# One GpSimd instruction instead of eight for the low part of a weight slot, in a two-block network on one Trainium2 core

## What is computed

```python
def rwkv7_time_mix(h, ...):
    hh = h_prev - h
    r = (h + hh * mu[0]) @ w_r
    k = (h + hh * mu[2]) @ w_k
    v = (h + hh * mu[3]) @ w_v
    g = sigmoid((h + hh * mu[5]) @ g1) @ g2
    ...

def swiglu_ffn(h, w_gu, w_down):
    gate, up = jnp.split(h @ w_gu, 2, axis=-1)
    return (jax.nn.silu(gate) * up) @ w_down

def reference(x, ...):
    x = first_block(x, ...)   # layer 0: rwkv7 + ffn; layer 1: differential attention + ffn
    return second_block(x, ...)  # layer 0: gla + spatial gating; layer 1: retention + pooling
```

## Time and profile before

| | |
|---|---|
| median of 3 runs | 2076.11 us (2075.34 to 2078.84) |
| the profiled execution | 2074.83 us, of which its span is 2072.8 us |
| TensorE (PE) busy | 1907.4 us, 92% |
| VectorE (DVE) busy | 811.7 us, 39% |
| ScalarE (ACT) busy | 764.0 us, 37% |
| GpSimd (POOL) busy | 776.3 us, 37% |
| mean granted TensorE clock | 0.972 of full speed |

### The profile page before, as it was taken

The page is one execution under the profiler, slowest core; times in us unless marked ns, Lnnn a source line. Parts: engine busy times, 40 slices in busy tenths (PEclk is TensorE's granted clock), DMA queues, the critical chain, the costliest instruction groups (busy, mean ns, idle before and its releaser), DMA issues.

```text
span 2072.8 us, 35505 instructions
## 1 busy us (share of the span) xinstructions
PE 1907.4 (92%) x14984; PEld 1563.6 (75%) x14984; DVE 811.7 (39%) x1297; ACT 764.0 (37%) x1046; POOL 776.3 (37%) x640
## 2 busy tenths in 40 slices
PE   5998988778999999999999799999999999989997
PEld 3666857667788888877677478888888877788876
DVE  5578433456332221017876532222102222423443
ACT  5776333433332222124256532222212323243232
POOL 3444400014434444435431144434445342334452
PEclk8999999998999999999999999999999999999998
DMA  5111100003233332322211023333223221132111
GB/s 173 62 34 61 40 3 4 3 24 103 62 102 101 90 93 97 112 76 92 71 52 42 13 80 91 101 101 96 96 97 97 82 82 41 41 107 82 62 61 62
DMA packets 192357, 149.58 MB, mean 72 GB/s; under 512 B 6890, under 2 KB 190401, under 8 KB 192228
## 3 DMA queue, kind: packets, MB, share of 16 engines
q1 hardware_dynamic: 192228, 147.68, 23.2%
HBM read 145.57 MB, written 2.10 MB: 71 GB/s over the span
## 4 chain that ended last, share of the span: by engine, by line
PE 73%; DVE 11%; issue 7%; ACT 6%; POOL 4%; DMA 0%; DVEq 0%; SPq 0%; ACTq 0%; POOLq 0%
PE psum L2686 20%; PE psum L2688 19%; PE psum L2687 19%; PE psum L2865 4%; POOL w_lo L1213 4%; ACT w_hi L1347 2%; PE psum L3164 1%; PE psum L3177 1%; DVE X_lo L1919 1%; DVE xf L2379 1%; DVE col L2428 1%; DVE tq L2399 1%; PE psum L3274 0%; PE psum L3057 0%; PE psum L3287 0%
## 5 line engine op out<-in xcount | busy, mean ns | idle before, releaser
L1213 POOL TENSOR_TENSOR w_lo<-weight_raw,w_hi 128x256 fp32r<-128x256 f32 (+5 forms) x597 | 731.0, 1257 | 1033.7 <-ACT w_hi L1347 1033.6
L2686 PE MATMUL psum<-X_hi,w_hi 128*128 128x512 f32 x1336 | 548.6, 411 | 33.0 <-DVE X_lo L1919 20.2
L2688 PE MATMUL psum<-X_hi,w_lo 128*128 128x512 f32 x1336 | 525.3, 393 | 0.0
L2687 PE MATMUL psum<-X_lo,w_hi 128*128 128x512 f32 x1336 | 524.8, 393 | 0.0
L1347 ACT ACTIVATE w_hi<-weight_raw 128x2048 fp32r<-128x2048 f32 (+1 forms) x136 | 252.9, 1860 | 294.5 <-PE psum L2688 294.4
L2686 PEld LDWEIGHTS psum<-X_hi,w_hi 128*128 128x128 f32 x1336 | 253.1, 189 | 112.5 <-issue 46.9
L2687 PEld LDWEIGHTS psum<-X_lo,w_hi 128*128 128x128 f32 x1336 | 253.5, 190 | 58.0 <-issue 8.9
L2688 PEld LDWEIGHTS psum<-X_hi,w_lo 128*128 128x128 f32 x1336 | 253.2, 190 | 55.0
L2686 PE MATMUL psum<-w_hi,X_hi 128*128 128x256 f32 x640 | 186.7, 292 | 10.3 <-POOL w_lo L1213 10.2
L2687 PE MATMUL psum<-w_lo,X_hi 128*128 128x256 f32 x640 | 182.3, 285 | 0.0
L2688 PE MATMUL psum<-w_hi,X_lo 128*128 128x256 f32 x640 | 182.1, 285 | 0.0
(11 more groups left out here) (473 smaller groups left out, 2593.1 us busy)
## 6 DMA issues: line engine op xcount, KB each, us to landing
weight_raw<-in_ffn_w_gu SPq DMA_DIRECT2D x88, 512.0 KB, 4.9
weight_raw<-in_l_w_in SPq DMA_DIRECT2D x45, 512.0 KB, 4.5
weight_raw<-in_ffn_w_down SPq DMA_DIRECT2D x40, 512.0 KB, 3.7
weight_raw<-in_kv_w SPq DMA_DIRECT2D x16, 512.0 KB, 4.4
weight_raw<-in_l_w_out SPq DMA_DIRECT2D x16, 512.0 KB, 4.4
weight_raw<-in_rw_w_o SPq DMA_DIRECT2D x12, 512.0 KB, 4.5
weight_raw<-in_rw_w_k SPq DMA_DIRECT2D x8, 512.0 KB, 6.7
weight_raw<-in_rw_w_r SPq DMA_DIRECT2D x8, 512.0 KB, 4.0
```

The costliest lines, as they stand in the source:

```text
L1213: ins = pool.tensor_tensor(l, r, h.bitcast(F32), ALU.subtract)
L2686: pe.matmul(ps, wh, xh, start=start, stop=False, skip_group_check=True)
L2687: pe.matmul(ps, wh, xl, start=False, stop=False, skip_group_check=True)
L2688: return pe.matmul(ps, wl, xh, start=False, stop=stop, skip_group_check=True)
```

## The change

`low_product`, slots 0 and 1, and slots 2 and 3 call `low` with `cut=False`:

```diff
             def low_product(name):
                 for i in range(sum(1 for q in PL.slots if q[0] == name)):
-                    low(PL.first_slot[name] + i)
+                    low(PL.first_slot[name] + i, cut=False)
...
-            low(0)
-            low(1)
+            low(0, cut=False)
+            low(1, cut=False)
...
             for n in range(2, 4):
-                low(n)
+                low(n, cut=False)
             for name in ("r", "g1", "v", "g2"):
                 low_product(name)
```

## The result

| | before | after |
|---|---|---|
| median, same comparison | 2075.73 us (4 runs, 2075.3 to 2078.84) | 2116.93 us (4 runs, 2114.01 to 2122.88) |
| ratio | | 1.0206, 95% interval 1.0182 to 1.0230 |
| profiled execution | 2074.83 us, span 2072.8 | 2115.84 us, span 2113.8 |
| TensorE busy | 1907.4 us | 1925.0 us |
| TensorE idle (span less busy) | 165.4 us | 188.8 us |

With a fourth run the median of the kernel before is 2075.73 us. The change costs 41 us, where +25.4 was forecast. The rows on TensorE split this: it idles 23.4 us longer, and it is busy 17.6 us longer with the same work, at a lower clock. The first is what the sum was about. The second I had weighed and left out of the sum.

The account below looks back on a forecast made before the run. The prediction took TensorE, 73% of the chain, as the bound nearly everywhere. Losses of 31.8 us less gains of 6.4 gave +25.4, so 2101.5 us against the median, range 2081 to 2114.

Parts of the forecast that it names:

- (a): Start: whole slots 0 and 1 and the low-rank weight hold VectorE, so TensorE's first product matmul comes later: +5.2 us.
- (b): Key product: slots 3 and 2 hold up VectorE's ring entries, for which TensorE waits: +2.4 and +1.0 us.
- (c): The r product, bound by VectorE: three slots hold it 12.6 us, largely given back by unslowed operations: +1.0 us.
- (d): The v product: the 5.17 us wait on GpSimd shrinks, but the third slot delays `kn_lo`: +3.4 us net.
- (e): The q product: the `X_lo` of k-tile 6 ends at 941.6, delaying its matmul: +3.6 us.
- (f): 956 to 1009 us, splits for kv and rotary embedding, set by VectorE: four slots hold it, +4.8 us.
- (g): Attention: three kv slots delay VectorE's softmax work, making it late for TensorE: +5.4 us.
- (h): Second block: `en_lo`, layer-norm statistics, a scaling and two smaller places lose time: +5.0 us.
- (i): Gains: some of TensorE's waits for a low part from GpSimd go or shrink: -6.4 us together.
- 5.2 version: At the start, both small constants are held up, giving +5.2 us; if the first slips through, 4.5.
- +8.5 makes +34: Upper bound: five new TensorE waits over 3 us, about 1.7 us of lowered clock each; left out of the sum.
- the waits grow, the clock follows: Rival, chance 0.20: clock drops and delays pass from VectorE to ScalarE to TensorE; 25.4 + 8.5 = +34, 2110 us.

Follow-up runs that it names:

- the two slots: Only the second `ega` and first `eo` slot, before the spatial unit, in one instruction each, against the kernel before: ratio 1.0057, +11.6 us in the mean.

## Why the prediction was wrong in size

The direction, the mechanism and the sum of the waits held: +25.4 forecast, +23.4 of idle time in the profile, +28.0 at equal clock over eight runs. What failed is the step that put the clock at nothing, below; and that the waits' sum is so near is in part luck. Term by term, from TensorE's idle time in the stretches of both profiles:

| term | forecast | found |
|---|---|---|
| (a), (b) start, key product | +8.6 | +9.0 |
| (c) r product, to the first v step | +1.0 | +5.7 |
| (d) v product | +3.4 | +1.3 |
| (e) q, first step | +3.6 | +3.1 |
| (f) to the rotary embedding | +4.8 | +5.4 |
| (g) attention | +5.4 | +4.5 |
| (h), (i) second block | -1.4 | -2.2 |
| stretches without a changed slot | 0 | -3.3 |

The stretches with changed slots give +26.8. The -3.3 comes from the recurrence core, whose 48.0 us of idle time in the profile of before is the longest of all profiles (42.0 to 47.0 in the others). Among the terms (c) is 4.7 too low, and (d) and (g) are 3.0 too high together. By the prediction's own numbers (d) is 215.4 - 212.2 = 3.2 and not 3.4, and (e) is 941.6 - 937.7 = 3.9 and not 3.6; the two slips nearly cancel.

- **(a)** The first product matmul came at 44.43, not 45.0. Both constants were held (3.25 and 4.40 us), as in the 5.2 version; the difference comes mainly from the three holds, which end at 36.3 instead of 37.1. The Trainium skill (SBUF — State Buffer, Who interferes with whom), by which a `tensor_scalar` in a 2-port mode is blocked as a two-input operation is, holds here: 3.25, 4.40, 3.04 and 4.76 us for operations with one tensor input in SBUF.
- **(c)** failed. I counted three slots that hold two-input operations, and their give-back. The first `v` slot stands in the same stretch and holds `sgf`, a `TENSOR_SCALAR`, for 3.04 us instead of 0.55, right before the chain that feeds the next step. VectorE is busy 4.2 us longer in the stretch, 2.5 of them by this operation. TensorE began the first `v` step without a wait before, and now waits 5.70 us there; before, then after:

```profile
189.38 0.36 PE L2686 MATMUL psum<-w_hi,X_hi 128*128 128x256 f32 x1
...
204.51 0.55 PE L2686 MATMUL psum<-w_hi,X_hi 128*128 128x256 f32 x1 [5.70 <-DVE X_lo L1919]
```

  The hold of `sgf` explains 2.5 of the 5.7. The rest was there before it: ScalarE, which feeds this chain, was 12.7 us behind the kernel before, and TensorE only 9.6, since its last wait ahead of it is shorter now (1.33 us at 175.29, not 2.78 at 164.10) and it takes 1.6 us less from there to the `v` product (23.5, not 25.1). The rule that I had quoted for the start applied here, and I didn't look for such operations elsewhere. The same holds in (h): `esv` 4.76 us, and `ymean` (128x4) 4.39 before the layer-norm.
- **(d)** As foreseen the wait on GpSimd goes, and one of 5.04 us stands before the key norms, up to the end of `kn_lo` at 230.16:

```profile
230.26 0.77 PE L2692 MATMUL psum<-kn_hi,heads_r 128*128 128x512 f32 x1 [5.04 <-issue]
```

  What I had too high is the rest of the old wait: 5.17 less a start 2.0 sooner is 3.2 us, and it is 1.4, since TensorE comes to the second step later, having waited at the first, (c). With the second `v` slot whole and the first in pieces it was 2.91.
- **(i)** The gain came, 5 us in the stretch from `elr` to `egb`.
- **The step that failed** is in the bounds: "+8.5 makes +34. I take the sum without it, as two old waits go." The term for the clock was put at nothing; it is +14.3 us over eight runs. Even my upper price was too low: 1.7 us for each of five waits over 3 us, from the earlier trace rows, where the clock was low for some 4 us. In the profile after, two places give 9.2 us (`q` to attention) and 9.5 us (the spatial unit) of the 17.6 us of extra busy time; the others cancel but for -1. In the spatial unit the clock averages 0.59 to 0.84 for 30 us behind a wait of 1.5 us:

```profile
1810.00:1815.00 5.00, 4.23 (x16) 3.06 (x16) 2.26 (x4) 0.00 (x0) 0.00 (x0) 0.73 0.64 210
1815.00:1820.00 5.00, 5.00 (x18) 3.93 (x17) 0.69 (x1) 0.60 (x1) 0.00 (x0) 0.59 0.01 3
...
1835.00:1840.00 5.00, 5.00 (x17) 3.87 (x16) 1.89 (x3) 0.00 (x0) 0.00 (x0) 0.66 0.00 0
```

  Before, the same work ran at 1.00 throughout (all seven 5 us stretches from 1762 to 1797). The unit mixes full matmuls with small ones of 128x128 behind transposes; TensorE has no gap there from 1815 on (5.00 us busy in 5.00), and yet the clock goes back and forth between its two levels, 2.4 and 1.2 GHz. The six profiles with the two slots whole and no fill all show 53 to 55 us busy there, six of the nine with them in pieces under 49 (45.4 in four). The other three of the nine have 52 to 53 us without any new wait there. The length of a wait doesn't tell either: the clock stayed at 1.00 behind 1.84 us in the profile of before and behind 3.59 in that of the two slots, and fell behind 1.53. So the new waits make the fall the rule where it was the exception, and what starts it stays open. A waiting TensorE is thus charged twice in many of its runs, and the second charge depends on what follows.
- The rival "the waits grow, the clock follows" (0.20) is what happened, but its clock term of 8.5 is little over half the real one, and the growing delays in (f) and (g) that it also named didn't come (9.9 found, 10.2 forecast). Its price of 2110 was nearest, and the measured 2116.9 lies above the range's 2114.

## What to carry to other kernels

Read the length of an instruction on one of two engines that hold each other up, as GpSimd and VectorE do here, as the wait that it can put on the other: count the operations behind it, the one-input ones and the tiny ones too, and cut it where the other engine feeds the bound. Make it whole only where the bound engine waits for it and the other one is idle; here that is 10 of 58 slots, worth 3 to 7 us, where all 58 cost 42. And price a new wait of TensorE as its length plus clock, taken from runs, since the clock part was a third of the total here, and in the kernel of the two slots larger than the waits themselves (7.3 and 4.3 us).

## What the runs showed that I had not expected

- An operation of 128x8 that took 0.59 us before took 4.40 us, one of 128x4 4.39 for 0.62, one of 128x2 3.45 for 0.68. The size of a held operation didn't matter in these rows.
- The same kernel's runs differ mostly by clock: the kernel before took 2063.36 us at 0.979 and 2085.60 at 0.968. A profile shows one draw. In the profile of before, TensorE ran at 0.50 from 255 to 265 us, and in that of the full change there was no such stretch. A comparison of two single profiles put a gain of 7 to 9 us there that no change had made. The Trainium skill (TensorE: Matmul & The Clock Gate, Part 1: The HAM clock gate) says that the gate isn't in step with the kernel's start, so that a kernel's count of slow matmuls varies from run to run; the scatter here agrees.
- Work with no use, put where TensorE would wait, made a kernel 9 us faster (+11.6 to +2.4). It wasn't tried on the full change or on the kernel before.
